# Two of the five modulation vectors of a dense stage summed as columns in the next norm

## The reference, cut to what matters

```python
c_act = jax.nn.silu(c)
for l in range(DEPTH):                       # DEPTH = 2
    mod = (c_act @ w_ada[l] + b_ada[l]).reshape(b, N_MOD, 1, D_MODEL)
    sh1, sc1, g1, sh2, sc2, g2, sh3, sc3, g3 = [mod[:, i] for i in range(N_MOD)]
    h = modulated_norm(x, norm_g[l, 0], sh1, sc1)       # rmsnorm(x, g) * (1 + scale) + shift
    x = x + 0.5 * g1 * swiglu(h, ffn_wg[l, 0], ffn_wu[l, 0], ffn_wd[l, 0])
    h = modulated_norm(x, norm_g[l, 1], sh2, sc2)
    m = attn_pool_mixer(h, ...) if l % 2 == 0 else short_conv_mixer(h, ...)
    x = x + g2 * m
    h = modulated_norm(x, norm_g[l, 2], sh3, sc3)
    x = x + 0.5 * g3 * swiglu(h, ffn_wg[l, 1], ffn_wu[l, 1], ffn_wd[l, 1])
```

## Time and profile before

| | us |
|---|---|
| median of three runs (1502.41 to 1505.34) | 1503.1 |
| the profiled execution | 1502.93 |
| its span, first to last instruction | 1501.1 |
| PE busy | 1410.7 (94%) |
| DVE busy | 898.0 (60%) |
| ACT busy | 619.5 (41%) |
| mean granted TensorE clock | 0.975 of full speed |

### The profile page before, as it was taken

How to read it: one execution, slowest core, us unless ns; L and a number is a source line. 1 busy time by engine, 2 the same in 40 slices (tenths; PEclk the granted TensorE clock), 3 DMA queues, 4 the chain that set the end, 5 groups by cost and what they waited for, 6 DMA issues and landing times.

```text
span 1501.1 us, 26991 instructions
## 1 busy us (share of the span) xinstructions
PE 1410.7 (94%) x11552; PEld 1263.5 (84%) x11552; DVE 898.0 (60%) x1044; ACT 619.5 (41%) x740; POOL 19.1 (1%) x24
## 2 busy tenths in 40 slices
PE   7999999989999999999999999999999989995666
PEld 5999999989999989999999999999997989762223
DVE  4877775657877768777776655556557644420002
ACT  3534345555434453443444544445434643420002
POOL 0000000400000000000000000000000000000000
PEclk9999999999999999999999999999999999998779
DMA  9998867516988758788655465553635439999996
GB/s 363 323 328 300 287 251 246 152 54 245 322 302 303 258 190 313 281 299 305 206 169 169 135 209 189 175 188 123 196 96 177 158 138 350 378 420 421 420 421 271
DMA packets 204056, 380.34 MB, mean 253 GB/s; under 512 B 12741, under 2 KB 158154, under 8 KB 192202
## 3 DMA queue, kind: packets, MB, share of 16 engines
q1 hardware_dynamic: 203616, 379.08, 70.3%
q10 hardware_dynamic: 362, 0.14, 0.0%
HBM read 378.14 MB, written 1.05 MB: 253 GB/s over the span
## 4 chain that ended last, share of the span: by engine, by line
PE 82%; DMA 9%; DVE 4%; ACT 3%; issue 2%; SPq 1%; DVEq 0%; ACTq 0%
PE ps L697 18%; PE ps L699 17%; PE ps L698 17%; PE ps L725 11%; PE ps L726 5%; DMA plain_whi<-in_w_exp_down_dram 4%; PE ps L1486 2%; ACT whi L1599 2%; DMA raw<-in_w_exp_down_dram 2%; DVE wlo L2051 1%; DMA spare<-in_w_exp_down_dram 1%; DMA plain_whi<-in_w_ada_dram 1%; PE ps L1460 1%; PE ps L1444 1%; PE ps L815 1%
## 5 line engine op out<-in xcount | busy, mean ns | idle before, releaser
L2051 DVE TENSOR_TENSOR wlo<-raw,whi 128x2048 fp32r<-128x2048 f32 (+2 forms) x187 | 423.1, 2263 | 226.8 <-ACT whi L1599 226.7
L1599 ACT ACTIVATE whi<-raw 128x2048 fp32r<-128x2048 f32 (+2 forms) x187 | 352.7, 1886 | 153.6 <-PE ps L699 138.0
L697 PE MATMUL ps<-h_both,whi 128*128 128x256 f32 x1320 | 380.1, 288 | 1.0 <-DVE wlo L2051 0.9
L699 PE MATMUL ps<-h_both,wlo 128*128 128x256 f32 x1320 | 374.5, 284 | 0.0
L698 PE MATMUL ps<-h_both,whi 128*128 128x256 f32 x1320 | 374.4, 284 | 0.0
L697 PEld LDWEIGHTS ps<-h_both,whi 128*128 128x128 f32 x1320 | 251.3, 190 | 8.7 <-issue 4.1
L725 PE MATMUL ps<-h_both,whi 128*128 128x512 f32 x704 | 252.3, 401 | 0.0
L698 PEld LDWEIGHTS ps<-h_both,whi 128*128 128x128 f32 x1320 | 251.5, 191 | 0.7 <-issue 0.5
L699 PEld LDWEIGHTS ps<-h_both,wlo 128*128 128x128 f32 x1320 | 251.5, 191 | 0.0
L697 PE MATMUL ps<-hidhi,whi 128*128 128x256 f32 x704 | 201.3, 286 | 2.1 <-DVE wlo L2214 2.1
L699 PE MATMUL ps<-hidhi,wlo 128*128 128x256 f32 x704 | 199.4, 283 | 0.0
(11 more groups left out here) (352 smaller groups left out, 1867.7 us busy)
## 6 DMA issues: line engine op xcount, KB each, us to landing
ada_raw<-in_w_ada_dram SPq DMA_DIRECT2D x66, 1024.0 KB, 5.3
raw<-in_ffn_wg_dram SPq DMA_DIRECT2D x44, 1024.0 KB, 6.8
raw<-in_ffn_wu_dram SPq DMA_DIRECT2D x44, 1024.0 KB, 5.4
raw<-in_ffn_wd_dram SPq DMA_DIRECT2D x44, 1024.0 KB, 6.4
raw<-in_w_in_dram SPq DMA_DIRECT2D x18, 1024.0 KB, 5.3
raw<-in_w_in_c_dram SPq DMA_DIRECT2D x12, 1024.0 KB, 5.3
raw<-in_w_in_ab_dram SPq DMA_DIRECT2D x8, 1024.0 KB, 8.6
raw<-in_w_exp_down_dram SPq DMA_DIRECT2D x7, 1024.0 KB, 16.7
```

Of the source, the lines that this page charges most:

```text
L697: pe.matmul(o, wh, xh, start=start, stop=False, skip_group_check=shared)
L699: return pe.matmul(o, wl, xh, start=False, stop=stop, skip_group_check=shared)
L1599: act.activation(whi[s][:, 0:width], raw[s][:, 0:width], ACT.Copy).then_inc(high[s], 1)
L2051: dve.tensor_tensor(wlo[s][:, 0:width], raw[s][:, 0:width], whi[s][:, 0:width].bitcast(F32), ALU.subtract).then_inc(split[s], 1)
```

## The change

Of the five vectors of ffn0, ffn1 and ffn2 the first three (`EARLY = 3`) are reduced as before. The weighted sums of the fourth and the fifth get tiles of their own (`adasum(3)`, `adasum(4)`) and are reduced in the norm after the stage: each by 8 matmuls with a 128x128 block of the weighted sums as the stationary operand and one column of ones as the moving one (`vector_columns`), which gives the vector as 8 columns at once; DVE adds the bias (`late_mod`). The fourth is multiplied into bank 6 ahead of the spread, in the place of `keep_clock(8)`, the fifth into bank 7 behind it, and bank 7 is then free when `mod_ready` says that the fifth is in `modv`. `fill` is 8 less there (6 for the mixers, 0 for ffn2). On DVE `late_mod` stands behind k = 3 and k = 4 of the norm. PE's loop of five pairs becomes two loops, of three pairs with a vector and two without; DVE's loop over vectors runs twice and the rest is written out. The norms ahead of ffn1, ffn3 and blk2 stay as they are.

```diff
-        adasum = ar(0, D)
+        EARLY, VECTORS = 3, 5
+        def adasum(i):
+            return ar(max(i - EARLY + 1, 0) * D, D) if isinstance(i, int) else ar(0, D)
...
+        reduced = {"ffn0": 0, "ffn1": 3, "ffn2": 6}
+        behind = {"ffn0": 0, "mix0": 2, "ffn1": 2, "ffn2": 4}
...
+            def vector_columns(v, i, b):
+                pe.wait_ge(ada_used[1], v * 2 + 2)
+                for j in range(KT):
+                    mm = pe.matmul(ps[:, b, T // 2 + j:T // 2 + j + 1], adasum(i)[:, j * P:(j + 1) * P], ones[:, 0:1], start=True, stop=True)
+                mm.then_inc(sem("adacol_ready"), 1)
...
-                keep_clock(8)
+                if late is None:
+                    keep_clock(8)
                 own(6)
                 pe.wait_ge(sem("mod_ready"), vectors)
+                if late is not None:
+                    vector_columns(late, EARLY, 6)
                 wait("norm_rs")
                 for j in range(4):
                     mm = pe.matmul(ps[:, 6, T + j * TQ:T + (j + 1) * TQ], ident[:, 32 * j:32 * j + 1].to_broadcast([P, P]), rstd[:, 0:TQ],
                                    start=True, stop=True)
                 mm.then_inc(sem("norm_spread"), 1)
                 freed[6] = (sem("t_ready"), KT * norms[0])
+                if late is not None:
+                    own(7)
+                    vector_columns(late + 1, EARLY + 1, 7)
+                    freed[7] = (sem("mod_ready"), late + 2)
+                    fill = max(fill - 8, 0)
                 keep_clock(fill)
...
-                    with pe.Fori(0, nv) as i:
+                early = 0 if layer_v is None else EARLY
+                if early:
+                    with pe.Fori(0, early) as i:
                         pair(i, i + layer_v)
-                if nv < pairs:
-                    with pe.Fori(nv, pairs) as i:
-                        pair(i)
+                with pe.Fori(early, pairs) as i:
+                    pair(i)
...
-            norm_sums(7, 14)
+            norm_sums(5, 14, late=5)
...
-            norm_sums(13, 0)
+            norm_sums(11, 0, late=11)
             chunked("ffn2", 13)
-            norm_sums(18, 14)
+            norm_sums(16, 14, late=16)
...
+            def late_mod(v, b):
+                dve.wait_ge(sem("adacol_ready"), v + 1)
+                sl = slice(v * KT, (v + 1) * KT)
+                dve.tensor_tensor(modv[:, sl], ps[:, b, T // 2:T // 2 + KT], bada[:, sl], ALU.add).then_inc(sem("mod_ready"), 1)
...
                 for k in range(KT):
                     scaled(k)
                     if k and not final and not after:
                         low(k - 1)
+                    if late is not None and k in (3, 4):
+                        late_mod(late + k - 3, 6 if k == 3 else 7)
```

More of the change, by code:

```diff
@@ L832, in first_norm_sums, with norm_sums @@
                 frees(7, "stat_read")
-            def norm_sums(vectors, fill):
+            def vector_columns(v, i, b):
[3 more added lines that the diff above has]
+                mm.then_inc(sem("adacol_ready"), 1)
+            def norm_sums(vectors, fill, late=None):
                 norms[0] += 1
@@ L871, in ada_quarter, with ada_turn @@
                 mm.then_inc(ada_used[i], 1)
-            def ada_turn(v):
-                pe.wait_ge(sem("adarow_ready"), v + 1)
+            def ada_turn(v, skipped=0):
+                pe.wait_ge(sem("adarow_ready"), v + (1 - skipped))
                 for b in range(2):
@@ L879, in ada_turn, with ada_reduce @@
                     freed[6] = (sem("mod_ready"), v + 1)
-            def ada_reduce(v, n):
+            def ada_reduce(v, i, n):
                 pe.wait_ge(ada_used[1], v * 2 + 2)
                 pe.wait_ge(sem("mod_ready"), v)
+                total = adasum(i)
                 for j in range(4):
-                    mm = pe.matmul(ps[32 * j:32 * j + 32, 6, 0:T], ones[:, 0:32], adasum[:, j * T:(j + 1) * T],
+                    mm = pe.matmul(ps[32 * j:32 * j + 32, 6, 0:T], ones[:, 0:32], total[:, j * T:(j + 1) * T],
                                    start=True, stop=True)
@@ L1002, in pair @@
                         if v is not None and half:
-                            ada_reduce(v, i + weighed[stage])
+                            ada_reduce(v, i, i + reduced[stage])
                         down(c, half)
                     if v is not None:
-                        ada_turn(v)
+                        ada_turn(v, behind[stage])
                 pairs = (count - 1) // 2
-                if layer_v is None:
-                    nv = 0
-                else:
-                    with pe.Fori(0, nv) as i:
+                early = 0 if layer_v is None else EARLY
+                if early:
+                    with pe.Fori(0, early) as i:
                         pair(i, i + layer_v)
-                if nv < pairs:
-                    with pe.Fori(nv, pairs) as i:
-                        pair(i)
+                with pe.Fori(early, pairs) as i:
+                    pair(i)
                 down(count - 1, (count - 1) % 2, last=True)
@@ L1147, in _ @@
             unit_half(4, 1, "sq_done")
-            ada_turn(7)
+            ada_turn(7, behind["mix0"])
             unit_half(5, 0, "sq_done")
@@ L2091, in ada_sum_rows, with ada_weigh @@
                 dve.tensor_copy(adarow[:, :], ps[:, 6, 0:T]).then_inc(sem("adarow_ready"), 1)
[L2093 removed]
+            def ada_weigh(v, i_, n, quarters):
+                total = adasum(i_)
                 for r in quarters:
@@ L2105, in ada_weigh @@
                         if k:
-                            ins = dve.scalar_tensor_tensor(out=adasum, in0=w, scalar=weight, in1=adasum, op0=ALU.mult, op1=ALU.add)
+                            ins = dve.scalar_tensor_tensor(out=total, in0=w, scalar=weight, in1=total, op0=ALU.mult, op1=ALU.add)
                         else:
-                            ins = dve.tensor_scalar(adasum, w, weight, None, ALU.mult)
+                            ins = dve.tensor_scalar(total, w, weight, None, ALU.mult)
                         ins.then_inc(ada_used[i] if kk else sem("ada_step"), 1)
@@ L2134, in _, with norm @@
             first_vector(0)
-            def norm(gain, shift, scale=None, final=False, vectors=0, inverted=False, slot=None, after=None):
+            def late_mod(v, b):
+                dve.wait_ge(sem("adacol_ready"), v + 1)
+                sl = slice(v * KT, (v + 1) * KT)
+                dve.tensor_tensor(modv[:, sl], ps[:, b, T // 2:T // 2 + KT], bada[:, sl], ALU.add).then_inc(sem("mod_ready"), 1)
+            def norm(gain, shift, scale=None, final=False, vectors=0, inverted=False, slot=None, after=None, late=None):
                 if scale is not None:
@@ L2228, in chunk @@
                         if quarters[0]:
-                            ada_weigh(part + vec, part + weighed[stage], quarters)
+                            ada_weigh(part + vec, part, part + weighed[stage], quarters)
                     if turn is not None:
-                        ada_sum_rows(turn + weighed[stage])
+                        ada_sum_rows(turn + reduced[stage])
                     if last:
@@ L2246, in chunked @@
                 chunk(0, 0, down=False, weigh=((0, front),) if nv else ())
-                looped = max(min(nv, pairs) - 1, 0)
+                looped = 0
                 if nv:
-                    with dve.Fori(0, looped) as i:
+                    with dve.Fori(0, EARLY - 1) as i:
                         chunk(i * 2 + 1, 1, weigh=((i, back),))
                         chunk(i * 2 + 2, 0, turn=i, weigh=((i + 1, front),))
-                    chunk(looped * 2 + 1, 1, weigh=((looped, back),))
-                    chunk(looped * 2 + 2, 0, turn=looped, last=(looped * 2 + 2 == count - 1))
-                    looped += 1
+                    for i in range(EARLY - 1, nv):
+                        chunk(i * 2 + 1, 1, weigh=((i, back),))
+                        chunk(i * 2 + 2, 0, turn=i if i < EARLY else None, weigh=((i + 1, front),) if i + 1 < nv else (), last=(i * 2 + 2 == count - 1))
+                    looped = nv
                 if 2 * looped + 1 < count:
@@ L2302, in _ @@
             add_output("ffn0", mod(0, 2), half=True, vectors=3)
-            norm(ng(0, 1), mod(0, 3), mod(0, 4), vectors=5)
+            norm(ng(0, 1), mod(0, 3), mod(0, 4), vectors=5, late=5)
             refill(2)
@@ L2399, in _ @@
             add_output("ffn1", mod(0, 8), half=True, vectors=9)
-            norm(ng(1, 0), mod(1, 0), mod(1, 1), vectors=11)
+            norm(ng(1, 0), mod(1, 0), mod(1, 1), vectors=11, late=11)
             refill(2)
@@ L2403, in _ @@
             add_output("ffn2", mod(1, 2), half=True, vectors=12)
-            norm(ng(1, 1), mod(1, 3), mod(1, 4), vectors=18)
+            norm(ng(1, 1), mod(1, 3), mod(1, 4), vectors=16, late=16)
             refill(2)
```

## The result

The changed kernel takes 1516.6 us (median of six runs, 1514.3 to 1519.2), the kernel before 1502.9 (six runs, 1502.4 to 1505.5). The ratio is 1.0088, with a 95% interval of 1.0073 to 1.0103: 13.7 us slower, where I had forecast 4.1, and outside my range.

A forecast was written before the change was run, and what follows sets the result against it. PE was taken to bound the kernel, busy for 1410.7 of 1501.1 us. The terms summed as 1502.93 - 3.8 (loops) + 1.6 (mixer gaps) + 2.5 (ffn2 gap) + 3.8 (clock) = 1507.0 us; range 1502.3 to 1509.5.

The forecast's parts named there:

- The loops, -3.8: In ffn0, ffn1 and ffn2, dropping two vectors' reductions saves 0.94 us in the loop and 0.32 in the tail per stage.
- The column products, 1.75 us: In the norm, each group of 8 column products takes 1.75 us; the first delays the spread by 0.50 us.
- The gaps without the clock, +0.8, +0.8, +2.5: Ahead of mix0, mix1 and ffn2, the added work delays PE by 0.8, 0.8 and 2.5 us at full clock.
- The bank wait: Ahead of ffn2, PE waits for bank 7 until DVE's second bias add, 0.7 us beyond PE's own path.
- my sum without the clock, +0.3: Loops and gaps together, -3.8 + 1.6 + 2.5: the gaps give back what the loops save.
- The clock, +3.8: One fall to half clock per gap: 1.5 us each ahead of mix0 and mix1, 0.8 ahead of ffn2; bounds 0 and 5.3.
- The row that I leaned on, L1522's: Four-column products kept PE busy for 3.72 us, then the clock was 0.50 from 1306.51 to 1309.90; cited for the falls.
- The Trainium skill's rule: The clock follows how busy PE has been recently, so a never idle PE keeps it; the sum would stay +0.3.
- 2 (the clock holds): In the three gaps the granted clock stays 1.00, so the kernel is not slower: 1503.2 us; chance 0.20.
- 5 (more room in the gap): Column products as short as the zeros replaced, clock held: 1501.2 us, below 1500 only with bank wait hidden; chance 0.04.
- 3 (two falls in one gap): Ahead of ffn2 a second slow stretch may follow the first, adding 1.5 us: 1508.5 us; chance 0.14.
- case 4: The second loop in three stages costs 0 to 1.8 us each for instruction fetch, 1509.7 us in the middle; chance 0.12.

The follow-up runs named there:

- experiment 2: Changed kernel with each group of 8 column products replaced by 15 zero matmuls of 256 columns, fourth and fifth sums left out, bank-7 wait kept; 2389.3 us, ratio 1.589.
- same_time_bias: Changed kernel with 15 wide zero matmuls for each group of column products, fourth and fifth vectors set to their bias, bank-7 wait kept; 1504.7 us, ratio 1.0006.
- same_time_nobank: Changed kernel with 15 wide zero matmuls for each group of column products, late sums left out, bank-7 wait removed; 1503.2 us, ratio 0.9999.
- zeros_behind: Complete changed kernel plus eight zero matmuls of 256 columns behind the first group of column products and eight more behind the second; 1517.7 us, ratio 1.0086.
- experiments 3 and 5: Changed kernel, late vectors bias alone: 15 wide zero matmuls per group of column products, 1504.7 us; column products kept with zeros as stationary block, 1516.3 us.
- loops_only: Changed kernel's loops with the earlier kernel's norm gap: no column products, late vectors bias alone, early bank-7 release; 1500.0 us, ratio 0.9979 to the kernel before.
- second_only: Changed kernel with the fifth vector's column products real, the fourth's replaced by 15 wide zero matmuls and its vector the bias; 1507.8 us, ratio 1.0034.

## Why the prediction was wrong, and where it was right

**The loops, -3.8: right.** ffn1 is 1.05 us shorter, against 1.26 forecast. ffn2 gave 1.40 back if its 5.12 is taken from the 6.52 that its gap costs (4.78 us later start of the gate product, 10.90 - 6.12, and a gate product that takes 7.88 us from 552.69 where it took 6.14). ffn0's last two chunks and tail are 1.28 shorter (DVE reads their up products 34.32 us apart in place of 35.27, and the tail takes 12.61 in place of 12.94). The other 0.8 of its 2.09 is there at ffn0's first up product already (46.83 against 47.62 us), ahead of any loop; that behind ffn3 some 0.8 us are lost is by all that the traces show a coincidence. Sum 3.7. DVE's up products read, in after, ffn1, the fourth and fifth pair:

```profile
494.86 0.69 DVE L2234 TENSOR_TENSOR act_tile<-act_tile,ps 128x512 f32<-128x512 f32 x1 [1.10 <-PE ps L705]
...
529.18 0.69 DVE L2234 TENSOR_TENSOR act_tile<-act_tile,ps 128x512 f32<-128x512 f32 x1 [1.10 <-PE ps L705]
```

34.32 us apart, as in ffn3, and 12.61 to the sums at 541.79, as I had forecast.

**The column products, 1.75 us: right at full clock** (1.81 us from 543.85 to 545.66), and the spread moved by what that says.

**The gaps without the clock, +0.8, +0.8, +2.5: right** (0.84, 0.81, 2.45 by experiment 2). The bank wait is there, 0.8 us. In the changed kernel itself it can't be seen: DVE adds the last bias at 550.68,

```profile
550.68 0.16 DVE L2161 TENSOR_TENSOR modv<-ps,bada 128x8 f32<-128x8 f32 x1
```

and PE's first gate product starts at 552.69, 1.9 us after that is done, because its zeros run at half the clock. So my sum without the clock, +0.3, is confirmed stage by stage: 0.84 + 0.81 + 2.45 - 3.7 = +0.4. The whole times agree with it less sharply: `same_time_bias` is 1.5 us over before, with one fall more inside mix0, and `same_time_nobank` is 0.3 over, though it lacks the bank wait and should lie 0.4 below; both intervals are about 1.5 us wide to either side.

**The clock, +3.8: the step that failed**, by its size. Its mechanism was right as far as it went: the column products keep PE busy and the clock falls, in each of the three gaps. The price of low clock was right too: I had 1.5 us for 3.4, and 3.1 for 6.9 and 4.7 for 10.2 are the same share, and ahead of ffn2 some 0.8 are swallowed by the bank wait, as I had it (4.7 - 0.8 = 3.9). Wrong was "one fall in each of the three gaps": they last 6.9, 10.2 and 10.2 us, eight lengths of 3.4 where I had three, and 11.7 us where I had 3.8. I had priced the cause at full clock and the fall as something that follows it and then is over. But the second group stands inside the fall and takes 3.38 us ahead of each mixer (233.41 to 236.79 and 753.88 to 757.26), in place of 1.81, and 2.66 ahead of ffn2, which keeps PE on narrow products while the clock is low. That two groups cost 11.9 and either alone 4.7 or 3.1 fits this. It can't be the whole of it: ahead of ffn2 the last narrow product is behind PE at 549.24, and the clock stays at 0.50 until 557.6, for 8.4 us of zeros with 128 columns and gate products; the 6.9 us of `zeros_behind` had no narrow product at all. What decides whether a fall lasts one, two or three lengths stays open. My upper bound for the term, 5.3, allowed a second stretch in one gap alone. With up to three in each gap it would have been 3 x 3 x 1.5 - 0.7 = 12.8 us, and the time of the slowest case 1502.93 + 0.3 + 12.8 = 1516.0.

The row that I leaned on, L1522's, was followed by one stretch of 3.4 us, and behind it stand products of 128 columns and more. I took its length from this one case, in which the cause was over when the fall began; `zeros_behind` shows that this alone doesn't make it short.

**The Trainium skill's rule.** PE was busy for all of 6.90 of the 6.90 us, 10.20 of 10.20 and 10.20 of 10.20, and the clock stayed at 0.50. The page "TensorE: Matmul & The Clock Gate" of the Trainium skill, section "What's actually happening", has the gate follow how busy the engine has been; read as busy time in a trace, that rule would have given 1503.2, and experiments 3 and 5 speak against that reading: with the same busy time, wide matmuls held the clock and narrow ones didn't, whatever they multiplied.

**The rivals.** 2 (the clock holds) is wrong, and so is 5 (more room in the gap): the column products took 1.81 us, not the 1.25 of the zeros that they replace. 3 (two falls in one gap) named the right direction and stopped too early. My range, 1502.3 to 1509.5, ended even below the middle of case 4, 1509.7, though I wrote that it left out only that case's far end. 4 (the second loop costs) falls: `loops_only` has the same second loop and is 2.9 us faster than before, and PE's longest wait for its own instructions stayed at 1.8 us in after (10.7 us in all, had 13.5):

```profile
PEld ps L703 <- issue: 10.7, 23, 1.8
```

## What to carry to other kernels

Judge an edit on TensorE by what it does to the clock as well as by its own length: a group of eight one-column products costs 1.8 us at full clock, and the six groups of this change cost 11.9 us more through the clock, 2.0 each. A fall must be priced with its length open: it lasted 3.4, 6.9, 10.2 and once 13.7 us here, and both ends belong into the range. Where a sum over partitions can be laid out with the data moving (256 columns against a stationary block of ones) or with the data stationary and one column moving, the first held the clock here, took PE no longer, and turned a loss of 13.7 us into a gain of 3.3.

## What I had not expected of the hardware

- The column products let the clock fall whatever they multiply: 1516.3 us with zeros as weights, 1516.6 with the weighted sums, 1504.7 with wide zeros of the same duration.
- Wide matmuls of zeros between one-column products did not hold the clock: 1521.2 us, with 10.2, 13.7 and 6.8 us at 0.50.
- A fall can last on without its cause: ahead of ffn2 in `zeros_behind` the clock was at 0.50 for 6.9 us that hold no narrow product.
- The same program loses a different amount to the clock in each execution: `second_only` took 1504.3 us at a mean clock of 0.977 and 1512.7 at 0.968.
- At half the clock a load of 128x128 weights with one moving column takes nearly twice its time, as a wide matmul does: 3.38 us for 16 records against 1.81, and 0.21 us against 0.12 for 256 columns.
